# Five gate panels set between the level products of a block inverse, memory heads moved into the recurrence, scatter of blocks later

## The reference

```python
proj = h @ a_w_in[i]
z, gate, q_mem, g_mem = jnp.split(proj, [A_SHIFT, A_SHIFT + BR_W, A_SHIFT + BR_W + MEM_W], axis=-1)
y_br = rwkv7_time_mix(z, ...)
...
def step(state, inp):
    r_t, w_t, k_t, v_t, kk_t, a_t = inp
    sa = jnp.einsum('bhvk,bhk->bhv', state, -kk_t)
    state = (state * w_t[:, :, None, :]
             + sa[..., None] * (kk_t * a_t)[:, :, None, :]
             + v_t[..., None] * k_t[:, :, None, :])
    y_t = jnp.einsum('bhvk,bhk->bhv', state, r_t)
    return state, y_t
...
s = jnp.einsum('bshd,bmhd->bhsm', q, k) * (HEAD_DIM ** -0.5)     # memory heads, 4 of them
p = jax.nn.softmax(s, axis=-1)
o = jnp.einsum('bhsm,bmhd->bshd', p, v)
...
y = jnp.concatenate([y_br * silu(gate), y_mem * silu(g_mem)], axis=-1) @ w_out[l]
```

## Time and profile before

| | us |
|---|---|
| median of 3 executions | 1318.83 |
| lowest, highest | 1318.52, 1320.29 |
| profiled execution | 1320.18 |
| its span, first to last instruction | 1318.4 |
| PE busy | 1213.6 (92%) |
| DVE busy | 845.1 (64%) |
| ACT busy | 631.4 (48%) |
| POOL busy | 198.6 (15%) |
| mean granted clock of PE | 0.965 |

### The profile page before, as it was taken

The page is one execution under the profiler, slowest core; times in us unless marked ns, Lnnn a source line. Parts: engine busy times, 40 slices in busy tenths (PEclk is TensorE's granted clock), DMA queues, the critical chain, the costliest instruction groups (busy, mean ns, idle before and its releaser), DMA issues.

```text
span 1318.4 us, 23948 instructions
## 1 busy us (share of the span) xinstructions
PE 1213.6 (92%) x9724; PEld 1163.2 (88%) x9724; DVE 845.1 (64%) x1452; ACT 631.4 (48%) x1081; POOL 198.6 (15%) x194
## 2 busy tenths in 40 slices
PE   6987879787997899999999999989999999999997
PEld 6976768587896899999999998889999999999997
DVE  5767954555665676665478764769656667877642
ACT  5766343444455564443344343653345445644442
POOL 2125320220001212120022100005100001122101
PEclk9989868988999989999999999999999999999999
DMA  6432310031442365555355542235545445755560
GB/s 251 150 109 96 97 64 1 33 128 65 158 131 96 128 237 180 175 166 173 120 160 160 170 157 91 97 112 176 173 168 170 130 143 178 235 183 188 159 196 32
DMA packets 53533, 185.78 MB, mean 141 GB/s; under 512 B 6704, under 2 KB 8880, under 8 KB 53168
## 3 DMA queue, kind: packets, MB, share of 16 engines
q1 hardware_dynamic: 52720, 180.97, 42.3%
q10 hardware_dynamic: 704, 3.29, 0.7%
HBM read 183.19 MB, written 1.05 MB: 140 GB/s over the span
## 4 chain that ended last, share of the span: by engine, by line
PE 72%; DVE 14%; ACT 9%; issue 3%; POOL 1%; DMA 1%; DVEq 0%; ACTq 0%; POOLq 0%
PE bank L2433 20%; PE bank L2436 20%; PE bank L2434 20%; DVE wl L1889 3%; ACT wh L1516 2%; PE bank L2448 1%; ACT L1493 1%; DVE zl L1981 1%; DVE sqr L1985 1%; PE bank L2568 1%; PE bank L2457 1%; ACT scb L1762 1%; DMA cols<-vecs 1%; DVE tmp L2346 1%; DVE tmp L2344 1%
## 5 line engine op out<-in xcount | busy, mean ns | idle before, releaser
L2433 PE MATMUL bank<-xh,wh 128*128 128x256 f32 (+1 forms) x2008 | 585.8, 292 | 21.1 <-DVE xl L2130 11.1
L2436 PE MATMUL bank<-xh,wl 128*128 128x256 f32 (+1 forms) x2008 | 575.9, 287 | 6.6 <-DVE wl L1889 6.5
L2434 PE MATMUL bank<-xl,wh 128*128 128x256 f32 (+1 forms) x2008 | 576.6, 287 | 0.0
L1889 DVE TENSOR_TENSOR wl<-raw,wh 128x1024 fp32r<-128x1024 f32 (+1 forms) x343 | 422.7, 1238 | 233.9 <-ACT wh L1516 232.4
L1516 ACT ACTIVATE wh<-raw 128x1024 fp32r<-128x1024 f32 (+1 forms) x343 | 356.1, 1044 | 309.4 <-PE bank L2436 297.7
L2433 PEld LDWEIGHTS bank<-xh,wh 128*128 128x128 f32 x2008 | 384.7, 192 | 30.7 <-issue 21.8
L2436 PEld LDWEIGHTS bank<-xh,wl 128*128 128x128 f32 x2008 | 386.4, 192 | 8.0 <-DVE wl L1889 8.0
L2434 PEld LDWEIGHTS bank<-xl,wh 128*128 128x128 f32 x2008 | 385.4, 192 | 0.6
L2433 PE MATMUL bank<-hh,wh 128*128 128x272 f32 (+1 forms) x352 | 100.3, 285 | 0.0
L2434 PE MATMUL bank<-hl,wh 128*128 128x272 f32 (+1 forms) x352 | 100.2, 285 | 0.0
L2436 PE MATMUL bank<-hh,wl 128*128 128x272 f32 (+1 forms) x352 | 100.2, 285 | 0.0
(11 more groups left out here) (362 smaller groups left out, 1568.1 us busy)
## 6 DMA issues: line engine op xcount, KB each, us to landing
raw<-w_ffn_gate SPq DMA_DIRECT2D x44, 512.0 KB, 3.6
raw<-w_ffn_up SPq DMA_DIRECT2D x44, 512.0 KB, 3.7
raw<-w_a_w_in SPq DMA_DIRECT2D x29, 512.0 KB, 3.5
raw<-w_ffn_down SPq DMA_DIRECT2D x32, 448.0 KB, 3.4
raw<-w_w_out SPq DMA_DIRECT2D x16, 512.0 KB, 3.5
raw<-w_b_w_in SPq DMA_DIRECT2D x16, 512.0 KB, 4.4
raw<-w_ffn_down SPq DMA_DIRECT2D x16, 512.0 KB, 3.6
raw<-w_ret SPq DMA_DIRECT2D x16, 512.0 KB, 3.5
```

The costliest lines, as they stand in the source:

```text
L1889: v.tensor_tensor(lo[:, c], raws[n % N_RAW][:, c], hi[:, c].bitcast(F32), ALU.subtract).then_inc(*w_lo.up(n))
L2433: pe.matmul(ps, hi[:, c], x_hi(k), start=(k == 0), stop=False)
L2434: pe.matmul(ps, hi[:, c], x_lo(k), start=False, stop=False)
L2436: last = pe.matmul(ps, lo[:, c], x_hi(k), start=False, stop=(k == kt - 1))
```

## The change

Three edits, all in `schedule()`, and one in ACT's program:

1. Among the lanes `fill()` now stops while more than 5 items are left, so five gate panels (20 to 24) are held back instead of four. `fill(2)` behind the lanes and the two fills in the recurrence are gone. The twelve steps of the levels are set by hand, with one `fill()` at five places among them, and `settle()` behind.
2. The memory heads of layer 0 leave the levels and are advanced step by step between the products of the recurrence.
3. ACT's scatter of the upper two blocks of the t form moves from `lanes_out` to `scatter`, where it stands ahead of the lower two, behind the third `lev_xt`. `ed_end` moves behind the levels.

No instruction of computation is added or removed; two of ACT's table loads go, because the last sigmoid now stands ahead of the first exponential.

```diff
--- before.py
+++ after.py
@@ -890,11 +890,9 @@
             do("lanes_in")
             for s in range(1, BLK - 1):
                 do("lane", s)
-                if len(between) > 4:
+                if len(between) > 5:
                     fill()
             do("lanes_out")
-            do("ed_end")
-            fill(2)
 
             def masked(c, kind):
                 for half in range(2):
@@ -938,8 +936,6 @@
                 do("lev_xt", n, b, freed)
                 bank.give(b, (xx_d, n), (xt_d, (n, 5)))
                 yield
-                if n == 2:
-                    do("scatter")
                 b, freed = bank.take()
                 do("lev_y", n, 6, b, freed)
                 bank.give(b, (yy_d, (n, 6)))
@@ -948,16 +944,25 @@
                 do("lev_t", n, b, freed)
                 bank.give(b, (xt_d, (n, 6)))
 
-            def heads(j):
-                for _ in memory_heads(0, j):
-                    yield
-                    yield
-
-            skewed([heads(0), levels(0), levels(1), levels(2), heads(1)])
+
+            lev = [levels(n) for n in range(3)]
+            for n in (0, None, 1, 0, None, 2, 1, 0, None, 2, 1, "scatter", 0, None, 2, 1, None, 2):
+                if n is None:
+                    fill()
+                elif n == "scatter":
+                    do("scatter")
+                else:
+                    next(lev[n], None)
+            settle()
+            do("ed_end")
+
+            head = [memory_heads(0, j) for j in range(2)]
             masked(0, "ak")
             step_w(0, "in")
+            next(head[0])
             masked(1, "ak")
             step_u(0)
+            next(head[0])
             masked(0, "rb")
             step_w(1, "in")
             b, freed = bank.take()
@@ -966,14 +971,17 @@
             bank.give(b, (st_d, BT - 1))
             bank.give(b2, (st_d, BT - 1))
             masked(0, "rk")
-            fill()
+            next(head[0])
             step_w(1, "state")
+            next(head[1])
             step_y(0)
+            next(head[0], None)
+            next(head[1])
             masked(1, "rb")
             step_u(1)
+            next(head[1])
             masked(1, "rk")
-            fill(5)
-            settle()
+            next(head[1], None)
             step_y(1)
 
             def group_norm(j):
@@ -1616,11 +1624,11 @@
                     for r in (0, 1):
                         last = s.activation(xx_m[quad[r], :, quad[r]], x_diag[quad[r], 0:24, :], ACT.Copy)
                     last.then_inc(*xts.up("x"))
+                elif kind == "scatter":
                     on.wait_ge(*ln_out.past("t"))
                     for r in (2, 3):
                         last = s.activation(xt_m[quad[r], :, quad[r]], blocks[quad[r], 0:24, :], ACT.Copy)
                     last.then_inc(*xts.up("high"))
-                elif kind == "scatter":
                     for r in (0, 1):
                         last = s.activation(xt_m[quad[r], :, quad[r]], blocks[quad[r], 0:24, :], ACT.Copy)
                     last.then_inc(*xts.up("low"))
```

## The result

The changed kernel takes 1312.57 us (median of 4 executions, 1311.26 to 1313.16). The kernel before, on the same chip, takes 1319.56 (4 executions, 1318.52 to 1321.25). The ratio is 0.9944, with a 95% interval from 0.9927 to 0.9962: 7.0 us faster. The forecast was 1310.3, the range 1304.5 to 1317.0.

The account below looks back on a forecast made before the run. TensorE, busy 92% of the span, was taken as the bound, losing time to waits and half clock. Group norm 7.6 us earlier plus 0.9 behind it gave 8.5 off the median 1318.83: 1310.3 us, range 1304.5 to 1317.0.

Parts of the forecast that it names:

- Part 1: Levels with panels 20 to 24 between their steps: idle time moved, not removed; levels end at 197.3 us.
- Level steps at full clock: The levels' small products without the panels: 9.0 us, between ends of 8.3 and 16.5.
- Wait of t for ACT's scatter: In level 0, a new wait for the upper scatter, now behind the third xt copy: 1.7 us.
- First slow stretch: Clock falls in the pause before the levels, so y5 and over half of panel 20 run slowly: 1.8 us.
- Second fall: Clock falls again between panels 22 and 23, where dense work is scarce: 3.1 us, ends zero and twice that.
- Part 2: Clock in the levels: falls in the 6.2 us pause, returns only on dense work; slow stretches cost 1.8 and 3.1.
- Rival (a): Levels: small products hold the clock up, the 3.1 us go: 1307.2, or 1304.5 with lucky phase; chance 0.18.
- Rival (b): Levels: first slow stretch is longer, panel 21 slow as well, 4 to 5 us: 1315; chance 0.14.
- Rival (c): Clock never rises in the levels: five panels cost 11.3 us more, levels 8.8: 1326; chance 0.06.
- Part 3: Recurrence: two panels leave (-6.1), heads enter (+6.0), three waits appear (+2.9): 42.3 us, ending at 239.6.
- Rival (d): Recurrence: the heads' softmax on ACT and DVE adds 7 to 10 us: 1317 to 1320, no change; chance 0.10.
- Part 4: Behind the recurrence: table load 0.1 us and w_out's first panel 0.8 gained, the latter guessed between -1.5 and +2.

Follow-up runs that it names:

- e8: Changed kernel with its five panels in a row behind the levels instead of between their steps: 1312.16 us.
- e1: Changed kernel with ACT's scatter of the upper blocks back in its early place, only the lower one late: 1308.87 us.
- e7: Changed kernel with three gate panels held back instead of five, two more running under the lanes: 1306.65 us.
- e2: Changed kernel with 14 unread filler products on PE in the long pause before the levels: 1312.98 us.
- e5: Kernel before with only the memory heads moved into the recurrence: 1316.38 us.
- e10: e9 with 10 unread filler products on PE in the pause before the levels: 1305.52 us.
- e4: Changed kernel with four gate panels held back instead of five, panel 20 running under the lanes: 1306.23 us.
- e6: e4 with the second pair of heads' scores issued behind y of the first chunk, their later steps also moved back: 1305.89 us.
- e11: Changed kernel with only the memory heads set back between the levels' steps: 1313.20 us.
- e12: Changed kernel with 3 unread filler products on PE in the wait for ACT's scatter, which stays late: 1309.78 us.
- e3: Kernel before with 16 unread filler products on PE in its pause before the levels' first xt: 1319.44 us.
- e9: e4 with the second pair of heads' scores issued ahead of the product with the state: 1304.94 us.

## Why the prediction was right, and where it was not

**Part 1, the levels.** From y5's start to the levels' end the sum had 30.1 us; the trace has 30.4. By terms:

- Idle before y5: 6.2 forecast, 6.34 measured. The pause was moved, as forecast, not removed.
- Five panels: 14.5 forecast. The three at full clock take 3.04 each with their edges (172.73 to 175.77), so 15.2; 0.7 short.
- Level steps at full clock: 9.0 forecast, some 10.7 measured (30.4, less 17.8 for the panels as they ran, less 1.55 of wait, less 0.4 for the slow y5). This is the term that was most wrong. I took y5's row as nearest and misread it: the trace has two records for each f32 product, so its x32 are the 16 products of one step, 0.69 us or 43 ns each, and not two steps at 22 ns. And no step halves: a y6 or t takes 1.07 us at full clock against 1.9 at half, and all twelve 10.7 against e8's 16.4.
- Wait of t for ACT's scatter: 1.7 forecast, 1.55 measured; shown by e1.
- First slow stretch: 1.8 forecast, 1.5 measured (y5 0.4, panel 20 4.14 against 3.04).
- Second fall: 3.1 forecast, 1.5 measured, all of it in panel 23 (4.55 us). It fell where it was expected and came back sooner. The reason given was little dense work for 4.5 us. What the runs show is that the idle time in it counts: e1, without it, has no fall, and e7 has none behind 3.8 us of small products with no idle time.

The errors, 2.4 too little and 2.1 too much, nearly cancelled. The levels end at 196.6, forecast 197.3; counted from L both are 71.5, so the 0.7 us is the start in front of the lanes.

**Part 2, the clock.** The Trainium skill (TensorE: Matmul & The Clock Gate, section "Why this matters for your kernels") wants no idle gap over about 3 us. The pauses of 6.34, 6.05 and 3.77 us agree; but in e2 the clock fell just behind a wait of 1.55 us, with PE busy for 16 us before it, so the rule is not enough here. Its other half, that 4 us of busy TensorE reach the fast clock, does not hold in e8, where PE was busy for 13.00 of 13.00 us at 0.50. The forecast said that the clock comes back only on dense work. It did so within panels here, but a panel is not needed: in e5 it came back between 198 and 199 us, behind 2.9 us of masked products (64x128) and in the 128x128 products that follow them. Rival (a), whose case rested on small products holding the clock, was right in that they hold it where no idle time stands among them (e1, e10) and wrong in that the change leaves one. Rival (b), a slow panel 21, did not come: it took 3.04 us. Rival (c), a clock that never rises in the levels, did not come either: it rose within panel 20. e8's levels are wholly at half clock, but its panels are mostly fast, so (c)'s price with five slow panels between the steps was measured by no run. Nor does its 8.8 us for the levels follow from its rows, which give 8.0 (16.5 less 9.0, and 0.5 for y5).

**Part 3, the recurrence.** 42.3 forecast, 41.8 measured (196.59 to 238.39). The heads' six groups take 6.0 us together, as forecast. Three waits of 2.64 us together came against 2.9, but not the same three: 0.43 for the first masks (1.1 forecast), 1.18 for the state's evacuation (1.4), none at the last masks (0.4), and one of 1.03 in front of mem_c behind the heads' exponentials, which I had called a sign against me. Rival (d) had that mechanism at seven to ten times its size.

**Part 4, the rest.** This term failed in sign: 0.9 us more gain forecast, 0.6 lost in the trace. Its guess of -1.5 to +2 us, for later falls that move in phase, does cover the loss. Up to w_out it went as forecast or better: its first panel came 8.9 us earlier, and the first product of its norm sums 10.1 (286.21 to 276.07). Timeline of PE at four places behind it, first in the kernel before, then in the changed one: scores of the differential attention, the first turn behind, memory turn of layer 1, norm sums of layer 1.

```profile
310.88 1.55 PE L2710 MATMUL bank<-kT,qT 64*128 64x128 f32 x8
...
336.91 0.38 PE L2457 MATMUL bank<-ta,tmp 128*128 128x128 f32 x2
...
414.61 0.60 PE L2673 MATMUL bank<-ta,mp 128*128 128x128 f32 x4
...
454.53 0.81 PE L2691 MATMUL bank<-sq,ta 128*128 128x256 f32 x3
```

```profile
299.99 0.93 PE L2718 MATMUL bank<-kT,qT 64*128 64x128 f32 x8
...
327.66 0.38 PE L2465 MATMUL bank<-ta,tmp 128*128 128x128 f32 x2
...
405.20 1.04 PE L2681 MATMUL bank<-ta,mp 128*128 128x128 f32 x8
...
446.15 1.03 PE L2699 MATMUL bank<-sq,ta 128*128 128x256 f32 x4
```

The lead is 10.9 us at the scores, 9.25 at the turn, 9.4 at the memory turn and 8.4 at the sums. Code that nobody touched takes 1.65 us more in one piece (27.67 against 26.03) and 1.0 more in another (40.95 against 39.92). Where the clock is low in the second, windows of the changed kernel and of e8 show:

```profile
409.00:425.00 16.00, 9.52 (x41) 6.81 (x42) 8.39 (x23) 10.15 (x23) 5.52 (x8) 0.50 0.00 1
```

```profile
409.00:425.00 16.00, 6.57 (x33) 4.13 (x32) 6.83 (x22) 12.33 (x32) 5.53 (x8) 0.74 0.02 8
```

The other traces show the same two lengths. From the scores to the turn the kernel before, e4, e5, e6, e7, e8 and e11 take 25.8 to 26.0 us (e12 26.1), the changed kernel, e1, e2, e3, e9 and e10 27.6 to 27.9. From the memory turn to the sums it is 39.8 to 39.9 for the kernel before, e4, e6, e7, e8 and e11, and 40.9 to 41.0 for the changed kernel, e1, e2, e3, e9 and e10 (e5 40.55, e12 41.4). So the 2.7 us that the changed kernel loses here come in steps, and neither its edit nor any of mine is in this code.

For the first step the rows say where. In all six traces with the longer piece the scores run at full clock (0.93 us) and in all eight with the shorter at half (1.54 to 1.66), so a trace with the clock down at the scores comes out shorter. Timeline of PE, the next product that waits for DVE, in the kernel before and in the changed one:

```profile
318.85 0.55 PE L2718 MATMUL bank<-ta,scb 128*128 128x128 f32 x3 [2.46 <-DVE scb L2188]
```

```profile
307.33 0.90 PE L2726 MATMUL bank<-ta,scb 128*128 128x128 f32 x3 [3.37 <-DVE scb L2196]
```

With scores at full clock PE is done sooner and waits for DVE longer, 3.36 to 3.38 us in all six, and behind that wait the clock has fallen (0.90 us for these products, and 0.51 from 306 to 313 us in the changed kernel). With scores at half clock it waits 1.21 to 2.66 us in all eight, and the clock is up (0.55 us, and 1.00 from 315 to 336 us in the kernel before). Why the clock is low at the scores in some traces and not in others, the runs do not show, and there is one trace of each kernel: whether the changed kernel always lies on the longer side is open.

**The sum.** Of the 8.2 us between the traces 8.15 come from the stretch and 0.7 from the front, by chance, and 0.6 are lost behind. The forecast of 8.5 had 7.6 in the stretch (0.5 too little), nothing in front, and 0.9 behind (1.5 too much); so against the traces it is off by 0.3 only, which is luck: 1.2 us in one direction and 1.5 in the other. The medians give 7.0 because the profiled execution before was 0.6 above the median of its four, and the one after 0.6 below. The 2.3 us between 1310.3 and 1312.57 are 1.5 (8.5 forecast, 7.0 in the medians), and 0.7 by which the kernel before measured higher in four executions than in three.

**A better version.** Four panels held back with the second scores early (e9, 1304.94 us, ratio 0.9895) or without (e4, 1306.23) beat both kernels; e4 is the simplest.

## What to carry to other kernels

Dense products set between small ones brought the clock back, and once (e4) covered a wait; in e8, at half clock, the copies of the levels cost nothing even without them. A fall behind one idle time was cheap where dense work followed soon (1.5 us); filling the idle time itself brought nothing where a second one stood behind it. Count a step that moves on a queue for what stands right in front of its user: here one scatter of 1.7 us, moved behind a copy, cost 3.3 us (its wait and the slow panel behind it), against the 8.15 that the whole change brought in its stretch. And a part of a schedule that has idle time is the place for the next panel even when the panel's other engine bounds that part: 1.5 to 1.9 us there against 3.0 in the levels. Last, faster work ahead of a wait for another engine makes the wait longer, and here the clock then fell behind it.
